# A decoder layer on one core: first expert stage fed in quarters, idle products, kept rows and the first projection blocks rearranged

## The chip, the cores and the metric

The kernel runs on one core of a Trainium2 chip. The metric is the device time of one execution in microseconds (us), as the median over several executions. TensorE is called PE here (its weight loads PEld), VectorE DVE, ScalarE ACT, GpSimd POOL and SyncE SP, as in the profile.

## What is computed

One decoder layer for 256 prompt tokens and 8 sample tokens, 264 together. All data are float32. Cut to what matters here:

```python
h = x + mixer(rmsnorm(x, norm_mix))            # one wide input projection w_in, SSD and short convolution
h = h + cross_attn(rmsnorm(h, norm_xattn), mem)
h = h + moe(rmsnorm(h, norm_moe))              # top 4 of 32 experts
y = rmsnorm(h, norm_final)

def moe(x):                                    # x is normed
    logits = x @ w_router + b_router
    top_v, top_i = top_k(logits, 4)
    gates = softmax(top_v)
    # per expert: gather its tokens, then
    gate, up = split(xb @ w_gate_up[e] + b_gate_up[e])
    y = ((clip(up) + 1) * gate * sigmoid(1.702 * gate)) @ w_down[e] + b_down[e]
    # scatter y * gate weight back to the tokens
```

The last three conv input rows and the sample rows of the projection are outputs too (`new_mconv`, `new_sconv`).

## The kernel before

Activations lie transposed, features on the partitions and the 264 tokens along the free axis: `hT` holds h, `xnT` its normed copy, each as 8 blocks of 128 features. A projection of 128 features is 8 matmuls of 128x264 into one PSUM bank (`project`, L1532); float32 makes two instructions of each. The order of the work on PE, ACT and DVE is written out by hand. `PLAN` (L51 to L93) lists every job of a bank with the engine that empties it; `filled`, `emptied` and `free_bank` turn it into waits.

**Start.** PE runs two idle matmuls of 512 columns (L1507), turns x block by block (a 128-row tile, the 8 sample rows, later the second 128-row tile), turns the parameter rows (`par0`) and spreads the root of the mean squares over the partitions with a product (`rbc`, L1492). DVE makes the sums of squares (L942) and scales the rows by `norm_mix` and the root (L959, `scale_rows`). Then come blocks `xb` 0 to 3, from a weight chunk of 2 MB that is fetched in halves, one from SP's queue (L477) and one from ACT's (L622).

**Router.** PE computes the attention's output projection `xo` in 8 blocks. After block j it adds the router's product of block j-1 (`route`) and turns the raw block back to tokens (`turn_tokens`). The last ones are followed by the sums of squares (`sum_tokens`), from which ACT and DVE make the root (L858, L1325); DVE then makes logits, the top four and a mask (L1329 to L1347). PE counts ranks with triangular products (`rank`, two idle products ahead and three behind, L1946), and in the same bank the total per expert, from which the number of passes follows (`npass`). DVE compares ranks with slot numbers (`select`, L1358): a selection matrix `selT` for 64 slots of each of two experts. `gather` multiplies it with the token rows `xtok` that ACT has scaled, ACT copies the result (`copy_rows`), PE turns it (`turn_rows`) and DVE multiplies by the gains `norm_moe` (`spread`, L1395), which gives `xg`, the stationary side of the expert's matmuls. Meanwhile six sets of four small turns bring out the kept rows (`mrow`, `srow`), which POOL writes to memory.

**Experts.** A pair of experts is 12 stages, one for each chunk of 2 MB: `gate_up(e, part)` four times for each expert, `down(e)` two for each. A stage is 16 matmul instructions of 64x512 columns and ends with an increment of `stage_done`. There are nine slots, so nine chunks (numbers 0 to 8) are fetched ahead. From then on SP fetches chunk after chunk, each when a stage has freed a slot:

```python
for g, done_stages in zip(range(AHEAD, AHEAD + 8), (1, 2, 3, 5, 6, 7, 8, 9)):
    sp.wait_ge(S["stage_done"], done_stages)
    refill(g, g // 12)
```

The slot of chunk 3 is used only once (it is work space later), so stage 4 is not in the list. Inside a pair PE also turns the activations, scatters the previous pair's result, and gathers, turns and biases for the next pair. Of the 16 pairs the first and the last are written out, and the 14 between run in a loop. After the last come a scatter, the final norm and the output.

The names in the rows: `flat` holds x and the parameter rows at the start, `tokT` is `hT` and `xnT`, `wide` is the work space, `ring`, `conv`, `flat`, `tokT` and a part of `wide` are the weight slots. L1492 is the helper for every product, L1503 the one for every turn, L618 and L609 ACT's copies.

## Time and profile before

| what | value |
|---|---|
| runs | 1410.58 us median of 3 (1409.34 to 1411.57) |
| profiled execution | span 1407.9 us; its time outside the span is not given |
| PE | 1376.7 us busy, 98% of the span |
| DVE / ACT / POOL | 441.5 / 217.9 / 27.9 us busy |
| memory read / written | 488.61 MB / 8.24 MB |
| chain that ended last | PE 83%, DMA 14%, DVE 2%, issue 1% |

The span runs from the first to the last instruction of the profiled execution. A busy share is an average over stages with different limits, so it does not name a bound. The chain is followed back from the last instruction, at each step to what released it. PE's records overlap, so the start of the next group is the better end of a group than its own busy time. In a timeline several like instructions in a row stand in one line with their count.

### The profile page before, as it was taken

Reading aid. Unit: us, or ns where it says so; the run is one execution under the profiler, and the core shown is the slowest. Engines: PE = TensorE matmul, PEld = TensorE weight load, DVE = VectorE, ACT = ScalarE, POOL = GpSimd, SP = SyncE. Lnnn points to the kernel's source line nnn. Section 1 sums busy time; section 2 is a strip of 40 time slices with the busy share of each in tenths; the row PEclk is TensorE's granted clock in tenths of the full one; section 3 lists DMA queues with packets and bytes.
Section 4 is the critical chain, followed back from the end, with each engine's and each line's share of the span. In section 5 each row is a group of like instructions: output and inputs, shape, how many; then the busy total and the mean of one; then the engine's idle time right before and its main releaser. Section 6 shows DMA issues by size and latency. Waiting matters only on the chain.

```text
span 1407.9 us, 16140 instructions
## 1 busy us (share of the span) xinstructions
PE 1376.7 (98%) x6438; PEld 673.5 (48%) x6438; DVE 441.5 (31%) x902; ACT 217.9 (15%) x403; POOL 27.9 (2%) x48
## 2 busy tenths in 40 slices
PE   9999999999999999999999999999999999999997
PEld 7788887677757633333333333333333332332322
DVE  5634345871461312221211312212113121121213
ACT  2220022052123411110101111011011010110102
POOL 0000002200000000000000000000000000000000
PEclk9999999999999999999999999999999999999999
DMA  7644446975379799999999999999999999999995
GB/s 256 210 154 154 175 142 200 376 268 190 118 283 398 284 413 428 429 425 430 427 430 427 430 427 429 428 429 429 428 428 429 430 427 430 427 430 426 431 426 228
DMA packets 71575, 497.25 MB, mean 353 GB/s; under 512 B 8752, under 2 KB 10216, under 8 KB 46824
## 3 DMA queue, kind: packets, MB, share of 16 engines
q1 hardware_dynamic: 65180, 477.94, 82.5%
q0 software_dynamic: 4432, 15.53, 3.0%
q10 hardware_dynamic: 1924, 3.23, 0.7%
q8 instruction: 27, 0.44, 0.1%
q14 instruction: 12, 0.10, 0.0%
HBM read 488.61 MB, written 8.24 MB: 353 GB/s over the span
## 4 chain that ended last, share of the span: by engine, by line
PE 83%; DMA 14%; DVE 2%; issue 1%; ACT 0%; SPq 0%; DVEq 0%
PE bank L1492 78%; DMA ring<-in_w_gate_up 8%; DMA flat<-in_w_gate_up 6%; PE bank L1503 4%; DVE wide L1418 1%; DMA flat<-in_x_prompt 0%; DVE wide L1475 0%; ACT wide L618 0%; PE bank L1946 0%; ACT L628 0%; ACT L658 0%; ACT wide L609 0%; SPq L506 0%; DVE wide L1466 0%; DVE wide L1395 0%
## 5 line engine op out<-in xcount | busy, mean ns | idle before, releaser
L1492 PE MATMUL bank<-ring,wide 128*64 128x512 f32 (+2 forms) x1696 | 405.5, 595 | 6.9 <-DMA ring<-in_w_gate_up 6.0
L1492 PE MATMUL bank<-wide 128*64 128x512 f32 (+6 forms) x1024 | 283.3, 574 | 8.7 <-DVE wide L1418 6.3
L1492 PE MATMUL bank<-tokT,ring 128*128 128x264 f32 x1152 | 266.0, 389 | 0.8 <-DVE tokT L959 0.8
L1492 PEld LDWEIGHTS bank<-ring,wide 128*64 128x64 f32 (+2 forms) x1696 | 132.4, 140 | 259.9 <-issue 246.1
L1492 PEld LDWEIGHTS bank<-tokT,ring 128*128 128x128 f32 x1152 | 217.8, 191 | 42.4 <-issue 6.4
L1492 PEld LDWEIGHTS bank<-wide 128*64 128x64 f32 (+4 forms) x1024 | 94.6, 152 | 171.9 <-issue 121.9
L609 ACT ACTIVATE wide<-bank 64x512 f32<-64x512 f32 (+3 forms) x104 | 58.2, 560 | 348.3 <-PE bank L1492 227.0
L1442 DVE TENSOR_SCALAR wide<-bank 128x512 f32<-128x512 f32 x32 | 22.1, 692 | 274.3 <-PE bank L1492 274.3
L1492 PE MATMUL bank<-flat,wide 128*64 128x512 f32 (+2 forms) x408 | 92.3, 589 | 3.7 <-DMA flat<-in_w_gate_up 3.7
L1492 PE MATMUL bank<-conv,wide 128*64 128x512 f32 (+1 forms) x400 | 91.1, 596 | 0.3 <-ACT wide L609 0.3
L890 ACT ACTIVATE wide<-wide 128x512 f32<-128x512 f32 x32 | 20.2, 630 | 428.6 <-DVE wide L1442 428.6
L1492 PE MATMUL bank<-tokT,wide 128*64 128x512 f32 x384 | 86.5, 592 | 0.0
L618 ACT ACTIVATE wide<-bank 128x264 f32<-128x264 f32 (+5 forms) x92 | 42.7, 482 | 210.3 <-PE bank L1492 179.2
L1492 PE MATMUL bank<-wide,ring 128*128 128x264 f32 x256 | 58.4, 386 | 0.5 <-ACT wide L609 0.5
L1492 PEld LDWEIGHTS bank<-flat,wide 128*64 128x64 f32 (+2 forms) x408 | 29.7, 137 | 59.7 <-issue 53.1
L1492 PEld LDWEIGHTS bank<-tokT,wide 128*64 128x64 f32 x384 | 27.6, 137 | 54.8 <-issue 54.8
L1418 DVE TENSOR_TENSOR wide<-bank,wide 8x512 f32<-8x512 f32 x32 | 21.8, 681 | 99.8 <-PE bank L1492 99.6
L1492 PEld LDWEIGHTS bank<-wide,ring 128*128 128x128 f32 x256 | 48.1, 190 | 9.1 <-ACT wide L609 0.7
L1492 PEld LDWEIGHTS bank<-conv,wide 128*64 128x64 f32 (+1 forms) x400 | 26.9, 135 | 53.2 <-issue 52.5
L1503 PEld LDWEIGHTS bank<-ident,wide 128*128 128x128 f32 (+4 forms) x252 | 31.7, 173 | 41.2 <-issue 39.8
L1423 DVE TENSOR_TENSOR wide<-bank,wide 128x512 f32<-128x512 f32 x64 | 44.2, 691 | 17.4 <-PE bank L1492 16.9
L1386 DVE COPY wide<-id 128x128 f32 (+1 forms) x16 | 3.6, 225 | 135.4 <-PE bank L1492 135.4
(257 smaller groups left out, 735.1 us busy)
## 6 DMA issues: line engine op xcount, KB each, us to landing
ring<-in_w_gate_up SPq DMA_DIRECT2D x64, 2048.0 KB, 26.1
ring<-in_w_down SPq DMA_DIRECT2D x32, 2048.0 KB, 28.1
flat<-in_w_gate_up SPq DMA_DIRECT2D x16, 2048.0 KB, 26.9
conv<-in_w_gate_up SPq DMA_DIRECT2D x16, 2048.0 KB, 25.5
wide<-in_w_gate_up SPq DMA_DIRECT2D x16, 2048.0 KB, 25.7
tokT<-in_w_gate_up SPq DMA_DIRECT2D x16, 2048.0 KB, 27.0
ring<-in_w_in SPq DMA_DIRECT2D x15, 2048.0 KB, 12.3
wide<-in_w_down SPq DMA_DIRECT2D x8, 2048.0 KB, 25.2
```

The source lines that it names most:

```text
L609: return s.activation(out, in_, ACT.Copy, scale=scale)
L618: done(s.activation(out, src, func), name, k)
L890: s.activation(sig[:, e, :], gate[:, e, :], ACT.Sigmoid, scale=ALPHA).then_inc(S["sig_ready"], 1)
L1386: v.tensor_copy(onehot[:, buf].rearrange("p (j c) -> p j c", j=2), bc(id4[:, bass.ds(pair * 2, 2)], CAP))\
L1418: ins = v.tensor_tensor(out=acc[0:TS, 2, 512 * h:512 * h + 512] if last else acc[rows, 2, 0:512], in0=bank[5 if last else 6][rows, :], in1 ...
L1423: return v.tensor_tensor(out=dst, in0=bank[j - 1 if last else 6 + j % 2][:, :], in1=dst, op=ALU.add)\
L1442: v.tensor_scalar(gate[:, e, :], bank[2 * e][:, :], LIMIT, None, ALU.min).then_inc(S["g_ready"], 1)
L1492: last[0] = pe.matmul(out, lhsT, rhs, start=start, stop=stop)
L1503: last[0] = pe.transpose(out, in_, ident[0:k, 0:k])
```

## The change

It keeps all results and moves or recasts these pieces:

- Start: a third idle product; the eight rows of `norm_mix` get a transfer, a turn and a copy of their own (`gain`), so that the scaling does not need `par0`; x is turned in blocks with all three tiles, four blocks before the root product and four behind; the second half of the first weight chunk goes through SP's queue; the first four blocks take the first half of the contraction each, then the second half each (`xb_first`).
- Sums: split in two, the part over blocks 0 to 6 before the last routings, the last block's behind; they now write three columns with unit vectors (`units`).
- Chunks 3 and 8 are fetched after `so` 3 and not after `xo` 7 and the sums; for this the squares `sqo` lie elsewhere, for which ACT waits for the v output ahead of its loop, and `gT` and `onehot` have moved.
- The bias products of the first pair, and idle products, fill PE's waits ahead of the ranks; the total has a bank and a place of its own, in the first pair.
- The first gather is a transposed one: `gather_turned` uses blocks of `xtok` as the stationary side and gives `xg` but for the gains, in four quarters of two blocks. One quarter precedes the first stage, three are put between stages 1 to 3. DVE's `spread_quarter` multiplies each by the gains. The other pairs gather as before.
- The kept rows are turned between stages 3 and 6, and the number of passes is loaded into registers behind the first pair.

```diff
-PLAN = [("xT", 8, A_), ("par0", 1, A_), ("rbc", 1, D_), ("xb", 4, A_), ("memT", 2, A_),
+PLAN = [("gain", 1, A_), ("xT", 4, A_), ("rbc", 1, D_), ("xT", 4, A_), ("par0", 1, A_), ("xb", 4, A_), ("memT", 2, A_),
...
-PLAN += [("xo", 5, D_, (0, 1)), ("xtok", 3, A_, (3, 4, 5)), ("xo", 3, D_, (1, 0)), ("mrow", 1, A_, (0,)),
- ("rt", 3, D_, (2, 6, 7)), ("rs", 1, A_, (1,)), ("xtok", 3, A_, (3, 4, 5)), ("mrow", 3, A_, (1, 6, 7)),
- ("srow", 2, A_, (0, 3)), ("rank", 1, D_, (2,))]
+PLAN += [("xo", 5, D_, (0, 1)), ("xtok", 3, A_, (3, 4, 5)), ("xo", 3, D_, (1, 0)),
+ ("rs", 1, A_, (0,)), ("rt", 3, D_, (2, 6, 7)), ("xtok", 3, A_, (3, 4, 5)), ("rank", 1, D_, (6,)),
+ ("total", 1, D_, (4,)), ("mrow", 4, A_, (5, 4)), ("srow", 2, A_, (5, 4))]
...
         if i == 0:
             sp.dma_start(dst[:, 0:4], src[:, 0:4]).then_inc(first_half, 16)
+            sp.dma_start(dst[:, 4:8], src[:, 4:8]).then_inc(slot_full[where], 16)
...
-    for j, name, k in ((2, "so", 1), (4, "so", 1), (5, "so", 3), (0, "so", 3), (1, "xo", 3), (3, "xo", 7)):
+    for j, name, k in ((2, "so", 1), (4, "so", 1), (5, "so", 3), (0, "so", 3), (6, "so", 3), (8, "so", 3), (1, "xo", 3), (3, "xo", 7)):
         filled(sp, name, k)
         first_chunk(FIRST_SLOT.index(j))
-    first_chunk(3)
-    filled(sp, "rs")
-    first_chunk(8)
     filled(sp, "xtok", 5)
     first_chunk(7)
-    sp.wait_ge(S["passes_ready"], 1)
-    n = sp.value_load(npass[0:1, 0:1], min_val=0, max_val=MAXP - 1)
...
     for g, done_stages in zip(range(AHEAD, AHEAD + 8), (1, 2, 3, 5, 6, 7, 8, 9)):
         sp.wait_ge(S["stage_done"], done_stages)
         refill(g, g // 12)
+    sp.wait_ge(S["passes_ready"], 1)
+    n = sp.value_load(npass[0:1, 0:1], min_val=0, max_val=MAXP - 1)
...
+    s.dma_start(stage[0:KB, 2, :], param_rows("norm_mix")).then_inc(gain_in, 16)
     for t, row, name, n in PARAM_ROWS[:6]:
         s.dma_start(stage[row:row + n, t, :], param_rows(name)).then_inc(par0_in, 16)
-    s.dma_start(mslot[0][:, 4:8], WEIGHTS[0][1][:, 4:8]).then_inc(slot_full[0], 16)
...
+    move("gain", 0, small[:, 302:310], KB)
...
-    for t, n in TILES_P:
-        copy(xtok[0:n, t, :], acc[0:n, t, :], rr[0:n, t:t + 1]).then_inc(S["xtok_ready"], 1)
-    for k in range(1, 4):
+    for h in range(2):
+        for t, n in TILES_P:
+            cols = slice(512 * h, 512 * h + 512)
+            copy(xtok[0:n, t, cols], acc[0:n, t, cols], rr[0:n, t:t + 1]).then_inc(S["xtok_ready"], 1)
+    s.wait_ge(S["lg_ready"], 1)
+    s.activation(gts, gts, ACT.Exp).then_inc(S["lg_exp"], 1)
+    for k in range(4):
         move("mrow", k, mrows[k // 2][:, k % 2 * 512:k % 2 * 512 + 512], 512, 11)
     for k in range(2):
         move("srow", k, srows[:, 512 * k:512 * k + 512], 512, 10)
-    s.wait_ge(S["lg_ready"], 1)
-    s.activation(gts, gts, ACT.Exp).then_inc(S["lg_exp"], 1)
...
+            if job == "rbc":
+                emptied(v, "xT", k)
+            ins = v.scalar_tensor_tensor(out=dst[:, k, 0:n], in0=src[:, k, 0:n], scalar=gain(k),
                                          in1=b[:, 0:n], op0=ALU.mult, op1=ALU.mult)
             if k < KB - 1:
                 ins.then_inc(S[out], 1)
...
-    st(ins)
+    done(ins, "rank")
+    emptied(v, "rank")
     v.wait_ge(S["consts_set"], 2)
     select(0)
...
+    def spread_quarter(q, gathered, ready):
+
+        v.wait_ge(S[gathered], q % 2 + 1)
+        v.tensor_tensor(out=xg[:, 2 * q:2 * q + 2, :],
+                        in0=bank[4 + q][:, 0:256].rearrange("p (k n) -> p k n", k=2),
+                        in1=bc(gains[:, 2 * q:2 * q + 2], P), op=ALU.mult).then_inc(S[ready], 1)
+
...
-    for _ in range(2):
+    for _ in range(3):
         pe.matmul(bank[7][:, :], ones[:], ones[:, 0:1].to_broadcast([P, 512]), start=True, stop=True)
...
+    pe.wait_ge(gain_in, 16)
+    b = free_bank(pe, "gain")
+    turn(b[:, 0:KB], stage[0:KB, 2, :])
+    close("gain")
+    for t in (2, 0, 1):
         pe.wait_ge(x_in[t], 16)
...
+    def turn_x(ks):
+
+        for k in ks:
+            b = free_bank(pe, "xT", k)
+            for t, (c, n) in enumerate(TILES):
+                turn(b[:, c:c + n], xtokin[0:n, t, k * P:k * P + P])
+            close("xT", k)
+
+    turn_x(range(4))
     b = free_bank(pe, "rbc")
...
+    turn_x(range(4, KB))
+    pe.wait_ge(par0_in, 16 * 6)
+    b = free_bank(pe, "par0")
+    turn(b[:, 0:P], stage[:, 0, :])
+    close("par0")
...
+    def xb_first():
+
+        for half in range(2):
+            if half:
+                chunk_in(pe, "xb0")
+            else:
+                pe.wait_ge(first_half, 16)
+            for j in range(4):
+                b = bank[BANK[JOB["xb", j]]] if half else free_bank(pe, "xb", j)
+                for k in range(4 * half, 4 * half + 4):
+                    if j == 0:
+                        x_normed(k)
+                    mm(b[:, 0:T], mslot[0][:, k, j * P:j * P + P], xnT[:, k, :], k == 0, k == KB - 1)
+                if half:
+                    close("xb", j)
...
+    def sum_early():
         b = free_bank(pe, "rs")
         pe.wait_ge(S["sq_summed"], 1)
+        for t, (c, n) in enumerate(TILES):
+            mm(b[0:n, 0:3], rinv[:, c:c + n], units[:, 3 * t:3 * t + 3], t == 0, False)
+
...
-        for t, (c, n) in enumerate(TILES):
-            mm(b[0:n, t:t + 1], rinv[:, c:c + n], ones[:, 0:1], True, False)
-            mm(b[0:n, t:t + 1], sqo[:, KB - 1, c:c + n], ones[:, 0:1], False, True)
+        b = bank[BANK[JOB["rs", 0]]]
+        for t in (2, 0, 1):
+            c, n = TILES[t]
+            mm(b[0:n, 0:3], sqo[:, KB - 1, c:c + n], units[:, 3 * t:3 * t + 3], False, t == 1)
         close("rs")
...
+    def stay_warm(b, n):
+
+        pe.matmul(b[:, 0:n], ident[:], bgu[:, 0:n], start=True, stop=True)
...
+        if j == KB - 1:
+            sum_early()
         if j:
             route(j - 1)
-            turn_tokens(j - 1)
-    pe.wait_ge(S["raw_kept"], 1)
-    cache_rows("mrow", 0, kept_x, 11)
+            if j < KB - 1:
+                turn_tokens(j - 1)
+    sum_last()
     route(KB - 1)
-    sum_tokens()
+    stay_warm(bank[1], 512)
+    turn_tokens(KB - 2)
     turn_tokens(KB - 1)
...
+    def gather_turned(h, blocks):
+
+        for i in blocks:
+            out = bank[4 + 2 * h + i // 2][:, i % 2 * P:i % 2 * P + P]
+            for t in (0, 1):
+                rows = xtok[:, t, 512 * h:512 * h + 512].rearrange("p (s d m) -> p s m d", d=P, m=2)
+                mm(out, rows[:, i // 2, i % 2, :], selT[:, t, :], t == 0, False)
+            rows = slice(32 * h, 32 * h + TS)
+            ends = xtok[rows, 2, 0:512].rearrange("p (s d m) -> p s m d", d=P, m=2)
+            mm(out, ends[:, i // 2, i % 2, :], selT[rows, 2, :], False, True)
...
     pe.wait_ge(S["crossed_in"], 96)
-    hidden_bias(first_pair, 0)
...
+    hidden_bias(first_pair, 0, (0,))
+    emptied(pe, "rt", 2)
+    stay_warm(bank[7], 512)
+    emptied(pe, "xtok", 3)
+    hidden_bias(first_pair, 0, (1,))
+    pe.wait_ge(S["mask_ready"], 1)
+    b = free_bank(pe, "rank")
...
+    close("rank")
+    stay_warm(bank[7], 512)
+    stay_warm(bank[7], 128)
+    emptied(pe, "xtok", 4)
+    pe.wait_ge(S["sel_ready"], 1)
+    pe.wait_ge(S["xtok_ready"], 3)
+    gather_turned(0, (0, 1))
+    last[0].then_inc(S["xg_gathered"], 1)
+    stay_warm(bank[7], 256)
...
+        if first:
+            pe.wait_ge(S["xg_quarter"], 1)
+            gate_up(0, 0)
+            emptied(pe, "xtok", 5)
+            gather_turned(0, (2, 3))
+            last[0].then_inc(S["xg_gathered"], 1)
+            emptied(pe, "rank")
+            pe.wait_ge(S["xtok_ready"], 5)
+            gather_turned(1, (0, 1))
+            last[0].then_inc(S["xgt_turned"], 1)
+            pe.wait_ge(S["xg_quarter"], 2)
+            gate_up(0, 1)
+            gather_turned(1, (2, 3))
+            last[0].then_inc(S["xgt_turned"], 1)
+            pe.wait_ge(S["xg_ready"], 1)
+            gate_up(0, 2)
+            b = free_bank(pe, "total")
+            for t, (_, r) in enumerate(TILES):
+                mm(b[:, 0:E], ones[0:r, :], msk[0:r, t], t == 0, t == 2)
+            close("total")
+            pe.wait_ge(S["raw_kept"], 1)
+            cache_rows("mrow", 0, kept_x, 11)
+            cache_rows("mrow", 1, kept_x, 11)
+            pe.wait_ge(S["xg_ready"], 2)
+            gate_up(0, 3)
+            cache_rows("mrow", 2, kept_x, 11)
+            cache_rows("mrow", 3, kept_x, 11)
+            gate_up(1, 0)
+            pe.wait_ge(S["cv_kept"], 1)
+            cache_rows("srow", 0, kept_cv, 10)
+            cache_rows("srow", 1, kept_cv, 10)
+            gate_up(1, 1)
...
     experts(first_pair, 0, 0, first=True)
+    pe.wait_ge(S["passes_ready"], 1)
+    n = pe.value_load(npass[0:1, 0:1], min_val=0, max_val=MAXP - 1)
```

PE at the start, before: the idle products, the turns and the root product, up to the first blocks.

```order
L1507 MATMUL bank<-ones 128x512 x2
L1503 MATMUL bank<-ident,flat 128x8
L1503 MATMUL bank<-ident,flat 128x128
...
L1503 MATMUL bank<-ident,flat 128x128 x10
L1492 MATMUL bank<-ident,rtok 128x128 x2
L1492 MATMUL bank<-ident,rtok 128x8
L1492 MATMUL bank<-tokT,ring 128x264 x32
```

The turns end with the parameter rows, and the root product follows them all.

PE at the start, in the changed kernel. The 8-row `stage` turn and the turns of `flat` by threes:

```order
L1527 MATMUL bank<-ones 128x512 x3
L1523 MATMUL bank<-ident,flat 128x8
L1523 MATMUL bank<-ident,flat 128x128 x2
L1523 MATMUL bank<-ident,flat 128x8
...
L1512 MATMUL bank<-ident,rtok 128x128 x2
L1512 MATMUL bank<-ident,rtok 128x8
L1523 MATMUL bank<-ident,flat 128x128 x2
...
L1523 MATMUL bank<-ident,flat 128x8
L1523 MATMUL bank<-ident,flat 128x128
L1512 MATMUL bank<-tokT,ring 128x264 x32
```

The root product stands between two groups of turns, and the parameter turn is last.

PE from the ranks to the first stages, before (`ustr` and `ones` products are the ranks and the total, `xgt` turns are `turn_rows`, `ring,wide` 64x512 are stages):

```order
L1946 MATMUL bank<-bgu,ident 128x256 x2
L1492 MATMUL bank<-wide,ustr 128x32
L1492 MATMUL bank<-wide,ones 128x32
L1492 MATMUL bank<-wide,ustr 128x32
L1492 MATMUL bank<-wide,ones 8x32 x2
L1492 MATMUL bank<-wide,ustr 8x32
L1492 MATMUL bank<-wide,ones 128x32 x3
...
L1492 MATMUL bank<-wide 128x512 x6
...
L1503 MATMUL bank<-ident,xgt 128x128 x8
...
L1492 MATMUL bank<-ring,wide 64x512 x24
L1492 MATMUL bank<-wide 64x512 x8
L1492 MATMUL bank<-ring,wide 64x512 x8
```

Six stages follow each other without other work.

PE at the same place in the changed kernel:

```order
L1986 MATMUL bank<-bgu,ident 128x512
L1986 MATMUL bank<-bgu,ident 128x128
L1512 MATMUL bank<-wide 128x128 x6
L1986 MATMUL bank<-bgu,ident 128x256
L1512 MATMUL bank<-ring,wide 64x512 x8
L1512 MATMUL bank<-wide 128x128 x12
L1512 MATMUL bank<-ring,wide 64x512 x8
L1512 MATMUL bank<-wide 128x128 x6
L1512 MATMUL bank<-ring,wide 64x512 x8
L1512 MATMUL bank<-wide,ones 128x32 x3
L1523 MATMUL bank<-ident,kept 11x128 x8
L1512 MATMUL bank<-wide 64x512 x8
```

The six 512-column products and eight turns are gone; 24 products of 128x128 stand for them, six of them ahead of the first stage and 18 between stages, where the total and the kept rows follow.

SP's queue from the first expert chunk to the first refill, before:

```order
L484 DMA ring<-in_w_gate_up 128x4096
L484 DMA flat<-in_w_gate_up 128x4096
L484 DMA conv<-in_w_gate_up 128x4096
L484 DMA ring<-in_w_gate_up 128x4096 x3
L484 DMA wide<-in_w_gate_up 128x4096
L484 DMA wide<-in_w_down 128x4096
L484 DMA tokT<-in_w_gate_up 128x4096
L501 TENSOR_LOAD npass
...
L506 DMA ring<-in_w_down 128x4096 x3
```

The two `wide` chunks (3 and 8) come behind all `ring` chunks but the refills.

SP's queue at the same place in the changed kernel:

```order
L486 DMA ring<-in_w_gate_up 128x4096
L486 DMA flat<-in_w_gate_up 128x4096
L486 DMA conv<-in_w_gate_up 128x4096
L486 DMA ring<-in_w_gate_up 128x4096
L486 DMA wide<-in_w_gate_up 128x4096
L486 DMA wide<-in_w_down 128x4096
L486 DMA ring<-in_w_gate_up 128x4096 x2
L486 DMA tokT<-in_w_gate_up 128x4096
L503 DMA ring<-in_w_down 128x4096 x3
```

The two `wide` chunks (3 and 8) stand ahead of the last two `ring` chunks, and the load of `npass` has left this place.

## Rows read from the trace of the kernel before

**Rows 1.** The page: transfer rate in 40 slices of the span.

```profile
GB/s 256 210 154 154 175 142 200 376 268 190 118 283 398 284 413 428 429 425 430 427 430 427 430 427 429 428 429 429 428 428 429 430 427 430 427 430 426 431 426 228
```

**Rows 2.** The chain of waits: start us, us, what.

```profile
558.43 0.99 PE bank L1492 x4
...
615.10 0.99 PE bank L1492 x4
...
1071.84 0.99 PE bank L1492 x4
...
1130.57 0.99 PE bank L1492 x4
...
1361.19 3.65 PE bank L1492 x16
```

**Rows 3.** Timeline of SP's queue: start us, us, then the instruction.

```profile
489.43 7.20 SPq L506 DMA_DIRECT2D ring<-in_w_down  x3
...
525.02 0.33 SPq L506 DMA_DIRECT2D wide<-in_w_gate_up  x1
```

**Rows 4.** Windows: PE, PEld, DVE, ACT, POOL busy; clock; DMA share; GB/s.

```profile
524.00:526.00 2.00, 2.00 (x12) 0.67 (x10) 0.00 (x0) 0.00 (x0) 0.00 (x0) 1.00 0.78 320
526.00:528.00 2.00, 2.00 (x12) 0.57 (x8) 0.00 (x0) 0.00 (x0) 0.00 (x0) 1.00 0.94 254
```

**Rows 5.** Timeline of the start, all engines.

```profile
1.08 3.78 PE L1507 MATMUL bank<-ones 128*128 128x512 f32 x4 [1.08 <-POOL ones L535]
...
5.71 0.38 PEld L1503 LDWEIGHTS bank<-ident,flat 8*128 8x128 f32 x2 [0.22 <-issue]
...
6.40 1.23 DVE L942 CUSTOM_DVE_ANT_0 conv<-flat 128x1024 f32<-128x1024 f32 x1
...
8.27 0.13 DVE L952 RECIPROCAL rtok<-rtok 8x1 f32<-8x1 f32 x1
...
13.45 3.29 DVE L959 SCALAR_TENSOR_TENSOR tokT<-tokT,par,bank 128x264 f32<-128x264 f32 x8 [5.05 <-PE bank L1492]
...
14.08 16.13 PE L1492 MATMUL bank<-tokT,ring 128*128 128x264 f32 x64 [0.76 <-DVE tokT L959]
```

**Rows 6.** Groups by form, PE, 14.1-17.6 us, then 18-30 us: busy us.

```profile
L1492 PE MATMUL bank<-tokT,ring 128*128 128x264 f32 x9 | 3.9, 610 | 0.8 <-DVE tokT L959 0.8
...
L1492 PE MATMUL bank<-tokT,ring 128*128 128x264 f32 x55 | 12.4, 386 | 0.0
```

**Rows 7.** Timeline of PE, routing to stage 6, and ACT's root.

```profile
467.33 0.68 PE L1492 MATMUL bank<-wrt,tokT 128*128 128x32 f32 x6
...
470.65 0.26 ACT L858 ACTIVATE wide<-bank,eps 128x2 f32<-128x2 f32 x1 [1.10 <-PE bank L1492]
...
471.10 2.64 PE L1503 MATMUL bank<-ident,kept 128*11 128x128 f32 x20
473.57 1.03 PE L1946 MATMUL bank<-bgu,ident 128*128 128x256 f32 x4
474.87 0.41 PE L1492 MATMUL bank<-wide,ustr 128*128 128x32 f32 x2 [0.27 <-DVE wide L1347]
...
476.02 0.96 PE L1492 MATMUL bank<-wide,ones 128*128 128x32 f32 x6
...
478.41 4.76 PE L1492 MATMUL bank<-wide 8*128 8x512 f32 x12
...
485.73 10.52 PE L1492 MATMUL bank<-ring,wide 128*64 128x512 f32 x48 [0.37 <-DVE wide L1395]
...
506.49 0.75 PE L1503 MATMUL bank<-ident,wide 128*128 128x128 f32 x4
```

**Rows 8.** One line, L477: issue ns, first and last start us.

```profile
L477 SPq DMA_DIRECT2D ring<-in_w_in x1: 429/429/429, 2.2 to 2.2; - x1
...
DMA to landing us min/median/max: 10.9/10.9/10.9
```

**Rows 9.** Timeline of PE, dense matmuls of 128x128.

```profile
212.36 3.84 PE L1492 MATMUL bank<-wide,flat 128*128 128x128 f32 x32
```

164 lines of the change are left out of this document (65 added, 99 removed).

## Prediction

> **What bounds the kernel now.** I read the page first: TensorE (PE) is busy nearly all the time and the transfer rate sits at 425 to 431 GB/s from about the middle of the program on [rows 1]. Two full resources at once say nothing about which one ends the program, so the chain of waits comes next. In the expert loop four marker rows of the chain give the length of one pair of experts: 615.10 - 558.43 = 56.67 us early and 1130.57 - 1071.84 = 58.73 us late [rows 2]. The early value is the PE's own length. The late one is the weights': a pair is 12 chunks of 2 MB, 25.17 MB, and 25.17 MB in 58.73 us is 428.5 GB/s, the plateau of rows 1; one chunk takes 4.894 us. So the transfers lose 2.06 us per pair against the PE, the nine chunks loaded ahead are used up after some eight pairs, and from then on a shift of the stream of transfers is a shift of the end. The last long stretch of PE work starts at 1361.19 on a chunk that had just landed [rows 2], with six chunks still to come: 1361.2 + 6 x 4.9 = 1390.6.
>
> What sets the stream's place? A chunk may be fetched when a stage (one chunk's worth of matmuls) frees its slot. Stage 1 frees the first at 489.43, stage 9 frees the eighth at 525.02 [rows 3]. Stage 1 would allow the eighth chunk to start at 489.43 + 7 x 4.894 = 523.69; it is allowed only at 525.02, 1.33 us later. The finely cut windows show that hole: 320 and then 254 GB/s from 524 to 528 where 429 is normal, (109 + 175) x 2 / 429 = 1.3 us lost [rows 4]. Check: 525.02 + 2.0 until data flows + 176 x 4.894 = 1388.4, and the last chunk was issued early enough that only the queue holds it. **So the end follows stage 9 of the first pair**, by up to 1.33 us it could follow stage 1 instead, and every later pair has 2.06 us more slack.
>
> **The change part by part.** The sum is made against the profiled execution, whose span is 1407.9 us; the median of the three runs is 2.7 us above that span, and I carry that difference unchanged. About 0.2% (2.8 us) is what a measurement of this kernel can tell from no change.
>
> *Start.* Between 14.08 and 30.21 the PE does 64 matmul instructions for the first four blocks [rows 5]. The first of them run at 3.9 / 9 = 0.43 us each, the rest at 12.4 / 55 = 0.225 us [rows 6]: 264 columns in the one and the other are TensorE's levels of 1.2 and 2.4 GHz. The column of the granted clock reads 1.00 for the whole stretch, so I go by the durations. Before the rise at about 17.8 the PE had run four warming instructions (1.08 to 4.9) and then transposes with gaps: 0.38 us of weight loads and 0.22 us idle for each pair of a 128-row and an 8-row turn [rows 5]. After 3.7 us of dense matmuls the rate doubled. The change puts a third warming matmul in (six instructions at 0.853 us, until 1.08 + 5.1 = 6.2) and ends it just where the second prompt tile is used (6.40 on VectorE, DVE). If the clock rises within this stretch and stays, the turns go at the 2.47 / 20 = 0.12 us that twenty turns take later, 471.10 to 473.57 [rows 7], about 0.48 us for a block's three; four blocks end at 6.5 + 1.9 = 8.4, just as the root is ready (8.27 + 0.13) [rows 5]; the root's product takes 0.7 (half of the 1.4 or so that it takes before DVE starts at 13.45); the other four blocks and the parameters end at 11.2. The scaling on DVE needs only the eight columns of the new small parameter transfer and starts about 9.3 instead of 13.45, so it is ahead. 64 instructions at 0.2225 us are 14.24: end at 25.5, 4.7 us earlier than 30.21. The bound on the other side is the weights: the first half chunk landed at 2.2 + 10.9 = 13.1 [rows 8]. If it does so again, the gain is 30.21 - 13.1 - 14.24 = 2.9. The other half no longer competes from ScalarE's (ACT's) queue but follows it on SP's, so I expect it near 11.5 and take **-4.2**, ends -2.9 and -4.7. The new split order (half the contraction for four blocks, then the other half) has 7.1 us of work before it needs the second half. SP issues one transfer more here, 0.43 us [rows 8], under transfers that are needed much later. From here to the router the chain is PE nearly without gaps, so I let the shift arrive whole.
>
> The Trainium skill (page "TensorE: Matmul & The Clock Gate", Part 1) says that half rate is the default state, that sustained activity lifts it, and that the same kernel reaches full rate after differing numbers of matmuls from run to run. The trace agrees with the first two parts (0.43, then 0.225 us). By the last part the median would lie between this case and the next, as no one profile decides.
>
> *Router to first stage.* I count from the routing matmuls at 467.33. ACT reads the row sums at 470.65, 3.3 us in [rows 7]; the change puts them ahead of the last routing block, one set of turns and one set of kept rows, so they are read about 2.0 in. From there to the first rank matmul lie 474.87 - 470.65 = 4.2 us, less one 0.18 us subtraction taken off DVE's chain: 6.1 in, about when the PE has done its bias products (moved here, about 1 us) and two warming matmuls. The ranks take 1.15 (474.87 to 476.02) and no longer share their bank with the total, 0.96 us [rows 7]; DVE needs 1.3 for ranks and selection (as before, 478.41 less the 477.1 at which it began): selection at 8.7. ACT's scaled rows are ready about 0.3 earlier, so they do not hold it. The gather changes form: six 512-column matmuls, copies on ACT, eight turns and two scalings, 478.41 to 485.73 or 7.3 us, become for the first weights a quarter of a transposed gather. 128x128 matmuls take 3.84 / 32 = 0.12 us an instruction [rows 9]; a quarter is 12, so 1.4 to 1.5, and its scaling 0.5 with its waits. The first expert matmul then stands 10.7 in, against 485.73 - 467.33 = 18.4: **stage 1 comes 7.7 us earlier**.
>
> Stage 9 still has all of that work before it. Before, stage 6 ends at 506.49 - 467.33 = 39.2. Now: 10.7, the six stages' 20.8 (485.73 to 506.49), three quarters of the gather (4.3), the total (0.8), 24 turns of kept rows (2.8), and five interruptions of the stream at about 0.2 (chosen; a switch between forms shows a tenth or two at each side): 40.4, or 1.2 late. From stage 6 to 9 nothing changes. If the interruptions are free and a quarter takes 1.2, it is 0.5 early; at 0.4 each it is 2 late. I take **+1.0**, ends -0.5 and +2.0.
>
> *Other pieces.* Two chunks (3 and 8) are asked for two projections earlier; by the argument above chunks before the eighth refill do not set the end: 0. If that cover is gone, the stage that waits for chunk 3 pays its landing, not seen before. The pass count is loaded to a register behind the first pair instead of ahead of it, on PE, ACT, DVE and SP. On PE it now lies between two pairs, under 2.06 us of slack; before, it fitted with the last turns and the scaling into the time to 485.73, so it is far below that: 0. ACT now waits for the v output before its first square; it is asked for before the sample's values are weighed, well ahead of the output projection, so I count 0; if it were late, everything behind would wait.
>
> **Sum:** -4.2 + 1.0 = -3.2: span 1404.7, runs **1407.4**.
>
> **The rivals.** *The clock does not rise at the start.* Four warming instructions did not lift it before; six may not. Then the turns keep 0.78 us a block, the products 1.4, and the PE reaches the weights at about 14.3; with 16.13 as before it ends 0.2 us later. With the router's +1.0 this is +1.2: 1411.8. For it: after the four instructions the turns ran at half rate all the same [rows 5]. Against: the stretch is half as long again, 5.1 us, and the rise at 17.8 came after no more dense work than that.
>
> *Stage 1 sets the stream.* If the interruptions cost nothing and the first pair closes up, stage 9 moves by its end of -0.5 or better by 1.5, and with the whole 4.7 in front the sum is -6.7: 1403.9. More than that only if the eighth refill did not need stage 9; the 1.3 us hole speaks against.
>
> *The pieces cost more than the gather they replace (slower).* Eight of the transposed gather's 24 matmuls, 16 instructions, use 8 rows. At the start an 8-row weight load is followed by 0.22 us of idle time [rows 5]. If each of the 16 pays this, 16 x 0.22 = 3.5 us come on top in the first pair, stage 9 is 4.5 us late and, with no clock gain (+0.2), the sum is +4.7: 1415.3. It decides, past 0.2%, as soon as the pieces cost 1.6 us more than I count and the start gains nothing. Against it: the 0.22 is a low-clock value, and half of it at full clock leaves 1413.5.
>
> **How the numbers follow.** Forecast 0.54 (own range 1405.0 to 1409.2, of it 0.37 beyond 0.2%, as its span crosses 1407.8); clock stays low 0.25 (0.24 within); stage 1 0.08 (faster); pieces 0.13 (0.12 slower). That gives faster 0.45, same 0.42, slower 0.13. The range 1404.0 to 1412.3 takes in the forecast and the low clock with 0.5 us of noise, and leaves out most of the last two, 0.18.
>
> **What would show it.** Start: the first 264-column matmul near 11.5 and all at 0.22 us; the fourth block done near 26 (at 30.4 the clock rival is right). Router: stage 1's refill 7 to 8 us nearer to the last routing block. Decisive: the refill by stage 9 at 525.0 - 4.2 + 1.0 = 521.8, the hole in front of it larger than 1.3 us, and the end moved by the same amount. If the end moves by another amount than this refill, the argument on the stream is wrong; if stage 9 is earlier than the start alone explains, the cost of the pieces is.

## The result, and the profile after

The changed kernel takes 1416.71 us (median of 5, 1415.01 to 1417.95) against 1410.58 of the kernel before (median of 5): ratio 1.0037, 95% interval 1.0026 to 1.0048. It is **slower by 6.1 us of medians** (5.2 by the ratio), where 3.2 faster was forecast and 1412.3 was the range's upper end. The profiled span is 1414.1 against 1407.9. From here on the run times of profiled executions are known too: they lie 1.9 to 2.1 us above their spans.

The page of the kernel after shows the plateau of [rows 1] again, 426 to 430 GB/s from the 17th slice to the last but one. The chain of waits of the kernel after (start us, us, what) answers to [rows 2]:

```profile
564.03 0.98 PE bank L1512 x4
...
620.70 0.98 PE bank L1512 x4
...
1078.01 0.99 PE bank L1512 x4
...
1136.77 0.98 PE bank L1512 x4
...
1367.38 3.65 PE bank L1512 x16
```

A pair is again 56.67 us early and 58.76 late; only the whole is shifted, the last stretch by 1367.38 - 1361.19 = 6.2 us. So the time is lost before the expert loop. The timeline of SP's queue after (start us, us, instruction), for [rows 3]:

```profile
483.90 14.06 SPq L503 DMA_DIRECT2D ring<-in_w_down  x3
...
530.62 0.33 SPq L503 DMA_DIRECT2D wide<-in_w_gate_up  x1
```

Stage 1 frees its slot 5.5 us earlier than before (489.43), stage 9 frees its own 5.6 us **later** (525.02), and the end went with stage 9. The windows around that refill (PE, PEld, DVE, ACT, POOL busy; clock; DMA share; GB/s), for [rows 4]:

```profile
528.00:530.00 2.00, 2.00 (x13) 0.59 (x10) 0.00 (x0) 0.00 (x0) 0.00 (x0) 1.00 0.69 295
530.00:532.00 2.00, 2.00 (x12) 0.70 (x10) 0.00 (x0) 0.00 (x0) 0.00 (x0) 1.00 0.59 115
532.00:534.00 2.00, 2.00 (x11) 0.49 (x7) 0.00 (x0) 0.00 (x0) 0.00 (x0) 1.00 0.70 238
534.00:536.00 2.00, 2.00 (x13) 0.91 (x13) 0.59 (x2) 1.19 (x2) 0.00 (x0) 1.00 1.01 434
```

Against 429 the hole is (134 + 314 + 191) x 2 / 429 = 3.0 us, where it was 1.3. What stage 1 allowed early is lost at once: all chunks ahead were in by then and the transfers stood nearly still from 480 to 484 (37 GB/s on average), had little to do again from 490 to 492 (123 GB/s), before stage 2 was done, and waited again here.

The start of the kernel after, timeline of all engines, for [rows 5]:

```profile
1.07 4.82 PE L1527 MATMUL bank<-ones 128*128 128x512 f32 x6 [1.07 <-POOL ones L534]
...
4.10 12.24 SPq L439 DMA_DIRECT2D wide<-in_mem_prompt  x2
...
6.54 2.13 PE L1523 MATMUL bank<-ident,flat 128*128 128x128 f32 x12 [0.50 <-DMA flat<-in_x_prompt]
...
11.98 14.51 PE L1512 MATMUL bank<-tokT,ring 128*128 128x264 f32 x64
...
28.52 1.58 PE L1523 MATMUL bank<-ident,wide 128*128 128x128 f32 x8 [2.03 <-DMA wide<-in_mem_prompt]
```

The start went as forecast in this profile: twelve turns in 2.13 us and 64 products in 14.51 (0.227 each), done at 26.5 instead of 30.2. (Whether the third warming matmul did it is another question, see "The start in the other profiles".) Then PE stands 2.03 us for the memory tokens, which SP's queue takes 12.24 us to issue, and the router's first row begins at 467.55, no earlier than the 467.33 of before.

The router and the first stages, timeline of PE after, for [rows 7]:

```profile
467.55 0.63 PE L1512 MATMUL bank<-wide,rinv 128*128 128x3 f32 x6
...
470.02 1.13 PE L1986 MATMUL bank<-bgu,ident 128*128 128x512 f32 x2
470.98 0.82 PE L1523 MATMUL bank<-ident,tokT 128*128 128x128 f32 x6
471.73 1.09 PE L1512 MATMUL bank<-bgu,wide 32*64 32x512 f32 x8
472.75 1.13 PE L1986 MATMUL bank<-bgu,ident 128*128 128x512 f32 x2
473.80 1.09 PE L1512 MATMUL bank<-states,wide 32*64 32x512 f32 x8
474.82 0.41 PE L1512 MATMUL bank<-wide,ustr 128*128 128x32 f32 x2
...
477.41 2.23 PE L1512 MATMUL bank<-wide 128*128 128x128 f32 x12
479.57 0.70 PE L1986 MATMUL bank<-bgu,ident 128*128 128x256 f32 x2
480.20 3.65 PE L1512 MATMUL bank<-ring,wide 128*64 128x512 f32 x16
483.79 4.45 PE L1512 MATMUL bank<-wide 128*128 128x128 f32 x24
488.17 3.65 PE L1512 MATMUL bank<-ring,wide 128*64 128x512 f32 x16
491.75 2.26 PE L1512 MATMUL bank<-wide 128*128 128x128 f32 x12
493.94 3.65 PE L1512 MATMUL bank<-ring,wide 128*64 128x512 f32 x16
497.52 0.96 PE L1512 MATMUL bank<-wide,ones 128*128 128x32 f32 x6
498.42 1.04 PE L1523 MATMUL bank<-ident,kept 128*11 128x128 f32 x8
```

The two halves of the bias products take 1.02 us each (471.73 to 472.75, 473.80 to 474.82); both together took 1.05 before (483.09 to 484.14). A quarter of the gather takes 2.16 (477.41 to 479.57), the other three 4.38 and 2.19. Stage 6 ends at 512.1, 44.5 us behind the first row, where it was 39.2.

### The profile page after: what moved, and what is told of

It is laid out like the page before. It is cut to its first block, busy times and chain, and to the rows that moved or that the text cites. A ratio compares the mean times of both kernels' runs of the same rounds, so it can differ in the third digit from the quotient of the medians.

```text
span 1414.1 us, 16187 instructions
## 1 busy us (share of the span) xinstructions
PE 1381.7 (98%) x6469; PEld 675.5 (48%) x6469; DVE 442.3 (31%) x906; ACT 217.8 (15%) x404; POOL 27.9 (2%) x48
## 4 chain that ended last, share of the span: by engine, by line
PE 82%; DMA 15%; DVE 1%; issue 1%; SPq 1%; ACT 0%; DVEq 0%
PE bank L1512 77%; DMA ring<-in_w_gate_up 8%; DMA flat<-in_w_gate_up 6%; PE bank L1523 4%; DMA wide<-in_mem_prompt 1%; DVE wide L1435 1%; SPq L439 1%; PE bank L1986 0%; DVE wide L1495 0%; ACT wide L617 0%; ACT L627 0%; ACT L658 0%; ACT wide L608 0%; SPq L429 0%; SPq L503 0%
## 5 line engine op out<-in xcount | busy, mean ns | idle before, releaser
L1512 PE MATMUL bank<-wide 128*64 128x512 f32 (+7 forms) x1066 | 288.3, 560 | 9.0 <-DVE wide L1435 6.3
L1512 PEld LDWEIGHTS bank<-wide 128*64 128x64 f32 (+4 forms) x1066 | 100.2, 153 | 173.1 <-issue 121.2
L1435 DVE TENSOR_TENSOR wide<-bank,wide 8x512 f32<-8x512 f32 x32 | 21.8, 681 | 100.4 <-PE bank L1512 100.2
L1474 DVE COPY wide<-bank 128x264 f32<-128x264 f32 x16 | 6.9, 433 | 122.6 <-PE bank L1523 122.6
## 6 DMA issues: line engine op xcount, KB each, us to landing
flat<-in_w_gate_up SPq DMA_DIRECT2D x16, 2048.0 KB, 27.2
ring<-in_w_in SPq DMA_DIRECT2D x15, 2048.0 KB, 12.2
```

The costliest lines, as they stand in the source:

```text
L1435: ins = v.tensor_tensor(out=acc[0:TS, 2, 512 * h:512 * h + 512] if last else acc[rows, 2, 0:512], in0=bank[5 if last else 6][rows, :], in1 ...
L1474: v.tensor_copy(gT, bank[4][:, 0:T]).then_inc(S["gT_ready"], 1)
L1512: last[0] = pe.matmul(out, lhsT, rhs, start=start, stop=stop)
```

## The experiments

Each was timed 5 to 12 times beside the kernel before, whose median was 1411.79 beside the first four, 1410.51 beside the next four (rows_side to kept_in_waits), 1410.89 beside three_costs and 1410.48 beside the other three; the ratios are taken against those runs, and a median in the table is not to be subtracted from 1410.58. Time and granted clock vary together: the twelve runs of start_only go from 1408.50 us at a mean granted clock of 0.999 to 1414.25 at 0.992. The marks below come from one profile each. Eight kernels (after, kept_quarter, rows_side, bias_whole, no_idle, kept_in_waits, ends_together, three_costs) do the same up to the root, and it stands at 467.76 to 470.63; so a mark by itself is uncertain by up to 3 us, and the distances between marks of one profile are what the readings rest on. "Root" is ACT's read of the row sums, "ranks" PE's first rank product, "S1" and "S9" the refills by stages 1 and 9, all in us of the profile.

| kernel | median | ratio to before, 95% | root | ranks | S1 | S9 | span | span - S9 |
|---|---|---|---|---|---|---|---|---|
| before | 1410.58 | | 470.65 | 474.87 | 489.43 | 525.02 | 1407.9 | 882.9 |
| after | 1416.71 | 1.0037 (1.0026, 1.0048) | 469.50 | 474.82 | 483.90 | 530.62 | 1414.1 | 883.5 |
| start_only | 1411.04 | 0.9994 (0.9983, 1.0005) | 469.42 | 473.64 | 488.20 | 523.78 | 1407.1 | 883.3 |
| router_only | 1416.08 | 1.0033 (1.0022, 1.0044) | 469.95 | 475.27 | 484.35 | 531.08 | 1414.1 | 883.0 |
| start_mem_act | 1411.49 | 0.9996 (0.9983, 1.0009) | 468.35 | 473.81 | 488.27 | 523.85 | 1407.1 | 883.3 |
| kept_quarter | 1415.39 | 1.0023 (1.0012, 1.0033) | 469.85 | 475.17 | 484.25 | 529.51 | 1412.7 | 883.2 |
| rows_side | 1415.01 | 1.0028 (1.0016, 1.0040) | 469.04 | 474.36 | 483.35 | 529.75 | 1412.8 | 883.1 |
| bias_whole | 1415.61 | 1.0037 (1.0024, 1.0050) | 470.63 | 474.76 | 483.84 | 530.56 | 1413.6 | 883.0 |
| no_idle | 1419.29 | 1.0065 (1.0053, 1.0078) | 470.38 | 474.44 | 487.32 | 534.04 | 1417.2 | 883.2 |
| kept_in_waits | 1415.44 | 1.0038 (1.0025, 1.0051) | 468.17 | 472.97 | 483.69 | 529.43 | 1412.4 | 883.0 |
| ends_together | 1414.04 | 1.0026 (1.0015, 1.0037) | 467.76 | 473.08 | 481.76 | 527.33 | 1411.2 | 883.9 |
| three_costs | 1411.44 | 0.9994 (0.9983, 1.0005) | 468.12 | 473.93 | 482.62 | 526.72 | 1409.9 | 883.2 |
| sums_first | 1409.92 | 0.9998 (0.9988, 1.0007) | 468.21 | 472.44 | 489.23 | 524.81 | 1407.9 | 883.1 |
| sums_first_mem | 1407.65 | 0.9984 (0.9972, 0.9996) | 466.71 | 471.79 | 486.25 | 521.83 | 1405.2 | 883.4 |

**What sets the end.** Read the last column first: over 14 kernels S9 ranges over 12.2 us and the span stays 882.9 to 883.9 behind it. S1 does not do that: in start_only and three_costs S1 is 5.6 us apart in one direction and the spans 2.8 in the other. These runs separate stage 9 from stage 1 but not from its neighbours, since S9 follows the end of stage 6 by 18.4 to 18.5 us in all of them; that it is stage 9 rests on the hole just before its refill. That it is the stream of transfers and not PE alone rests on the late pairs, 58.76 us against PE's own 56.67.

### The two halves of the change

start_only is the kernel before with the change's start, router_only the changed kernel without it. Of the pieces exchanged, as start_only has them:

```diff
-            for _ in range(2):
+            for _ in range(3):
...
+            pe.wait_ge(gain_in, 16)
...
+            turn_x(range(4))
...
-            xb(0, 1, 2, 3)
+            xb_first()
...
-            s.dma_start(mslot[0][:, 4:8], WEIGHTS[0][1][:, 4:8]).then_inc(slot_full[0], 16)
```

> The start of the change alone, on the router and the first pair of before. Theory A (the four blocks end 3.7 us earlier, but the memory tokens land at 28.5 and the turns that follow wait for them, and the block behind them runs at the lower clock again): every marker from 60 us on stands 0.2 us later than before, time within 1 us of before (1410 to 1412). Rival (the start does give 3 to 4 us and the router takes 9 to 10): 1406.5 to 1407.5.

> All of the change but its start. Theory A: the refill by stage 9 comes 5.4 us later than before and so does the end, 1415.5 to 1417. Rival (a large part of the 6.1 us is the start's): below 1413.5.

router_only carries the loss: 4.3 us by its median against the runs beside it (1416.08 and 1411.79), a ratio of 1.0033 where the whole change has 1.0037, and 6.2 us of span. Its S9 is 6.1 us later in time and, as expected, 5.4 counted from the router's first row (468.00). start_only is 0.75 us faster by its median, and its interval takes in no change; its profile has S9 1.2 us earlier. Timeline of PE in start_only:

```profile
12.19 14.41 PE L1496 MATMUL bank<-tokT,ring 128*128 128x264 f32 x64
28.78 1.09 PE L1507 MATMUL bank<-ident,wide 128*128 128x128 f32 x8 [2.19 <-DMA wide<-in_mem_prompt]
```

The same stop as in the changed kernel. Before, PE came to these turns at 30.05, when the memory tokens had landed; now it is there at 26.6 and they are not.

### The start in the other profiles

The new start stands in 12 of the 14 kernels. Timeline of PE at the start, before, then router_only (which has the old start and its two warming matmuls), then bias_whole (new start, three):

```profile
5.14 6.81 PE L1503 MATMUL bank<-ident,flat 8*128 8x8 f32 x25 [0.28 <-DMA flat<-in_x_prompt]
...
4.98 4.76 PE L1519 MATMUL bank<-ident,flat 8*128 8x8 f32 x24
...
15.60 15.97 PE L1512 MATMUL bank<-tokT,ring 128*128 128x264 f32 x64
```

In router_only two warming matmuls were followed by turns at full rate (24 in 4.76 us, where 25 took 6.81; a weight load of 0.14 us from 5.56 on, where before shows 0.18), and the clock was back at 0.50 from 9 us to 19. In bias_whole, no_idle and rows_side three warming matmuls did not hold it: PE waited 1.6, 1.6 and 0.7 us for the prompt (but 0.96 in kept_quarter, where the clock stayed at 1.00), the clock fell to 0.50 at 8 to 10 us, and the fourth block ended at 31.4, 31.2 and 29.8. In the other nine it ended at 26.3 to 27.2. So the full rate came in nine profiles of twelve and half rate, as the clock rival has it, in three, and no run takes the third warming matmul alone: that it lifts the clock is not shown. The landing of the memory tokens is why it hardly matters: rows_side ended its four blocks 3.3 us behind the changed kernel and has its root 0.5 us ahead of it (469.04 against 469.50).

### The memory tokens on another queue

```diff
-                        sp.dma_start(memv[t], a["mem_prompt"][0, t * P:(t + 1) * P, :].rearrange("p (a n) -> p a n", a=4))\
-                            .then_inc(mem_in, 16)
...
+                s.dma_start(memv[t], a["mem_prompt"][0, t * P:(t + 1) * P, :].rearrange("p (a n) -> p a n", a=4))\
+                    .then_inc(mem_in, 16)
```

> start_only with the two transfers of the memory tokens moved from SP's queue, behind two weight chunks, to ACT's. Theory A (what takes the start's gain is the landing of the memory tokens): they land well before 26.5, the four blocks end near 26.5, PE goes on at the full clock and the end is 3.5 to 4 us earlier than before, 1406.6 to 1407.1. Rival (the memory system gives no more bytes by then, whatever the queue: the next chunk is late instead): gain under 1.5 us, with PE waiting for the second chunk.

Here `sp` is SP's queue, where they stood behind the first weights, and `s` ACT's, where they stand behind the parameter rows. Missed in the median, met by the lowest of 12 runs alone (1406.71); by its median the rival is nearer, with the wait for `wdt` in place of the one for a chunk. The stop at 26 us is gone, a smaller one takes its place, 1.42 us for `wdt` at 36.7. The root stands 2.30 us earlier than before against 1.23 in start_only, so the memory tokens were worth 1.07 there. Behind it the ranks came 5.46 us after the root instead of 4.22, with the granted clock at 0.50 from 470 to 472, so 1.2 us went again. Why the clock fell is not shown: PE was busy 1.88 of the 2 us before.

### What stage 9 has ahead of it

kept_quarter leaves out three quarters of the kept rows:

```diff
-                for i in range(4):
+                for i in range(1):
                     turn(b[0:n, i * P:i * P + P], src[:, 4 * k + i, :])
```

> The changed kernel with one turn of four in each of the six sets of kept rows (the other three quarters of those output rows are left out): 18 turns fewer between stages 3 and 6 of the first pair, 18 x 0.12 = 2.2 us. Stage 1 keeps its place. Theory A (the eighth refill, by stage 9, sets the end): refill and end both 2.2 us earlier than in the changed kernel, 1414.5. Rival (stage 1 or an earlier refill sets the end): the end does not move, 1416.7.

From the ranks to S9 it is 54.34 against 55.80: 1.46 us less, of 2.2 expected. The turns take 1.19 us instead of 2.90 (two sets of one turn still cost 0.32, the first two 0.55), and 0.26 comes back as a wait for DVE at the end of stage 6. S1 kept its place (1.46 of S9 - S1 as well) and the span went with S9. By the runs alone this would not be shown: the intervals of the ratios (1.0012 to 1.0033, and 1.0026 to 1.0048 for the changed kernel) overlap, and so do those of rows_side, bias_whole, kept_in_waits and ends_together; there too the marks carry the reading. Those of no_idle and three_costs lie clear.

rows_side asks whether the strided weight load makes the gather's products slow:

```diff
-                    copy(xtok[0:n, t, cols], acc[0:n, t, cols], rr[0:n, t:t + 1]).then_inc(S["xtok_ready"], 1)
+                    copy(side(xtok[0:n, t, cols]), apart(acc[0:n, t, cols]), rr[0:n, t:t + 1]).then_inc(S["xtok_ready"], 1)
...
-                        rows = xtok[:, t, 512 * h:512 * h + 512].rearrange("p (s d m) -> p s m d", d=P, m=2)
+                        rows = xtok[:, t, 512 * h:512 * h + 512].rearrange("p (s m d) -> p s m d", d=P, m=2)
```

> The changed kernel with ACT writing the scaled token rows in the order in which the transposed gather reads them, so that each 128x128 weight block is contiguous instead of every second element; same result. A quarter of the gather is 12 instructions and took 2.16 us (0.18 each) where 128x128 products in the input stage take 0.12. Theory A (the strided weight load is what makes it 0.18): a quarter takes 1.5 us, the first stage comes 0.7 us earlier, stage 9's refill 2.6 us earlier counted from the last routing block, and the end moves by the same: 1416.7 - 2.6 = 1414.1. Theory B (0.18 is the price of a 128-column weight load with only 128 columns streamed behind it and of the switches of output, whatever the stride): the quarter stays 2.16 and the time 1416.7. Ends: if ACT's permuted reads are slower than its plain ones, the first stage is late by up to 0.5 us.

Theory B, nearly: a quarter takes 2.08 instead of 2.16, the whole gather 8.41 instead of 8.73. The stride is worth 0.3 us, not 2.6. (Ranks to S9 is 55.39, 0.4 less; the last 0.1 lies behind stage 6.)

ends_together changes the order, and with it the flags that open and close the sum in a bank:

```diff
-                for i in blocks:
-                    out = bank[4 + 2 * h + i // 2][:, i % 2 * P:i % 2 * P + P]
+                outs = [bank[4 + 2 * h + i // 2][:, i % 2 * P:i % 2 * P + P] for i in blocks]
+                for i, out in zip(blocks, outs):
...
-                        mm(out, rows[:, i // 2, i % 2, :], selT[:, t, :], t == 0, False)
+                        mm(out, rows[:, i // 2, i % 2, :], selT[:, t, :], i == blocks[0] and t == 0, False)
+                for i, out in zip(blocks, outs):
...
-                    mm(out, ends[:, i // 2, i % 2, :], selT[rows, 2, :], False, True)
+                    mm(out, ends[:, i // 2, i % 2, :], selT[rows, 2, :], False, i == blocks[-1])
```

> The changed kernel with the products of the transposed gather in another order: in each call the 128-row products of all its blocks first and then the 8-row products of all its blocks, so that the row count changes twice a call and not twice a block; same result. In the changed kernel six instructions of a block take 1.09 us, with 0.11 between like ones and 0.2 at each change of the row count. Theory A (the change of row count is what costs): a block is 0.2 us cheaper, a quarter 1.76 instead of 2.16, the first stage 0.2 to 0.4 and stage 9's refill 1.6 us earlier counted from the last routing block: 1415.1. Theory B (the eight-row instructions cost 0.3 us each wherever they stand): a quarter stays at 2.16, 1416.7.

Timeline of PE in ends_together:

```profile
475.67 1.84 PE L1512 MATMUL bank<-wide 128*128 128x128 f32 x12
477.44 0.70 PE L1986 MATMUL bank<-bgu,ident 128*128 128x256 f32 x2
...
481.65 3.67 PE L1512 MATMUL bank<-wide 128*128 128x128 f32 x24
485.26 3.65 PE L1512 MATMUL bank<-ring,wide 128*64 128x512 f32 x16
```

**Theory A, in the marks.** A quarter takes 1.77, two take 3.61 instead of 4.38, ranks to S9 54.25, 1.55 less than 55.80 for eight changes between 128 and 8 rows less: 0.19 us each. (The median is 1414.04, of 1415.1 expected.) In the changed kernel the eight blocks change 16 times: 48 instructions at 0.115 are 5.5 us, 16 changes 3.1, together 8.6 of the 8.7 measured. The Trainium skill (page "TensorEngine Tiling (Array Packing)", Key Properties) says that changing the tiling mode, not just the tile, drains TensorE. It gives no price, and that an 8-row weight block is such another mode is a reading that no run here shows; the 0.19 us does not speak against it.

### What stands ahead of the ranks

```diff
-            hidden_bias(first_pair, 0, (0,))
             emptied(pe, "rt", 2)
             stay_warm(bank[7], 512)
             emptied(pe, "xtok", 3)
-            hidden_bias(first_pair, 0, (1,))
+            hidden_bias(first_pair, 0)
```

> The changed kernel with the bias products of both experts in one call again, at the later of the two places. Theory A: the two halves take 1.02 us each, as much as both together before, and the second stands in front of the ranks, so the ranks, the first stage and stage 9's refill all come 1.0 us earlier: 1415.7. Theory B: the ranks wait for the mask that DVE makes, not for PE; then they move by less, 0.3 us or nothing: 1416.5.

Root to ranks is 4.13 against 5.32: 1.19 us less, and all of it arrives at S9, counted from the root. Timeline of PE in bias_whole:

```profile
473.72 0.66 PE L1512 MATMUL bank<-bgu,wide 32*64 32x512 f32 x4
473.74 0.66 PE L1512 MATMUL bank<-states,wide 32*64 32x512 f32 x4
...
474.76 0.41 PE L1512 MATMUL bank<-wide,ustr 128*128 128x32 f32 x2
```

The products of the two experts start 0.02 us apart, and 16 instructions take 1.04 us (473.72 to 474.76) where 8 alone take 1.02: they run side by side. By the kernel each of the eight products has its own 32 of the rows and 64 of the output columns. Split into two calls, with an idle product between, they did not overlap. (The median is 1.1 lower as well, but the ratio is the same 1.0037: in this profile the start ran at half rate and the root stands 1.1 us later.)

no_idle removes all five `stay_warm` calls of the changed kernel. kept_in_waits keeps the first and puts kept rows in the place of three, with banks 7 and 5 for them:

```diff
-            stay_warm(bank[7], 512)
+            pe.wait_ge(S["raw_kept"], 1)
+            cache_rows("mrow", 0, kept_x, 11)
             emptied(pe, "xtok", 3)
...
-            stay_warm(bank[7], 512)
-            stay_warm(bank[7], 128)
+            emptied(pe, "xtok", 5)
+            cache_rows("mrow", 1, kept_x, 11)
...
-            stay_warm(bank[7], 256)
```

> The changed kernel without its five idle products between the routing and the first stage. Theory A (the idle products are in PE's way: the two 512-column ones take 1.13 and 1.05 us where PE would otherwise wait for less): ranks, first stage and stage 9's refill come 1.3 us earlier, 1415.4. Theory B (they keep the clock up): without them the granted clock falls in the waits and the first stage runs at half rate, 3 us and more later: 1419 or above, visible as 0.43 us and more an instruction of 64x512 at twice that.

> The changed kernel with two of the six sets of kept-row turns put back into PE's waits, one in place of the second idle product, one in place of the third pair, and the 256-column idle product behind the first quarter dropped. Theory A (stage 9's refill sets the end, and useful work outside the waits is what the change added to it): two sets less between the stages are 1.0 us, a set is 0.5 us shorter than the idle product that it replaces ahead of the ranks, so the first stage comes 0.5 and stage 9's refill 1.5 us earlier: 1415.2. Theory B (the first stage sets the stream): only 0.5: 1416.2.

no_idle met its theory B. The ranks come 1.26 us sooner behind the root (4.06), and then (windows of no_idle, the clock is the last column but two):

```profile
474.00:476.00 2.00, 1.22 (x12) 0.99 (x12) 0.58 (x5) 2.00 (x4) 0.00 (x0) 0.93 0.99 422
476.00:478.00 2.00, 0.97 (x4) 0.93 (x4) 1.05 (x5) 1.98 (x3) 0.00 (x0) 0.50 1.00 426
...
484.00:486.00 2.00, 2.00 (x8) 0.67 (x6) 0.00 (x0) 0.00 (x0) 0.00 (x0) 0.51 0.00 0
486.00:488.00 2.00, 2.00 (x11) 0.82 (x8) 0.00 (x0) 0.00 (x0) 0.00 (x0) 1.00 0.00 0
```

PE waited 1.07 us before the ranks and 1.37 behind them, and with that second wait the clock goes to 0.50, the level of 1.2 GHz, for about ten microseconds; the first stage takes 5.86 us instead of 3.59. The idle products of the change are not waste: without them the median is 1419.29 and the ratio 1.0065. But they do not always hold the clock, as three_costs shows below. kept_in_waits showed the same in a smaller dose and no theory of mine had it: ranks 0.5 us sooner as expected, then waits of 0.84 and 0.52 us around the first quarter, and the first stage at the lower clock:

```profile
475.56 2.23 PE L1513 MATMUL bank<-wide 128*128 128x128 f32 x12 [0.84 <-DVE wide L1367]
478.31 5.34 PE L1513 MATMUL bank<-ring,wide 128*64 128x512 f32 x16 [0.52 <-DVE wide L1397]
```

That took 1.7 us, more than the 1.0 the two sets give back: ranks to S9 56.46, and the ratio stayed at 1.0038.

### Three costs at once

three_costs has the edits of bias_whole, ends_together and kept_quarter together.

> The changed kernel with three costs taken out at once: the bias products in one call, the gather's 8-row products together at the end of each call, and one kept-row turn of four in each set (this leaves out three quarters of the kept rows). Counted from ACT's root of the router to stage 9's refill, the three alone gave 1.2, 1.55 and 1.45 us off 61.1. Theory A (they stand one behind the other on PE, which sets stage 9, and stage 9 sets the end): together 4.2 off, 56.9, and with a span 883.3 above the refill's time the median comes to 1416.7 - 4.2 = 1412.5. Theory B (a wait on DVE, ACT or the clock comes in their place when all are gone, or the first stage begins to set the stream): 2 to 3 off, 1414.

From the ranks to S9 it is 52.79: 3.01 less than 55.80, exactly the 1.55 of ends_together and the 1.46 of kept_quarter. Root to ranks was 5.81, not 4.13, because the granted clock was 0.50 from 470 to 472 in the profiled execution (two idle products of 512 columns took 1.73 us where they take 1.13), although the idle products were there and PE's records show no gap from 466 on (up to 468.6 they are products of 264, 3 and 32 columns, as in the other kernels). The median is 1411.44, 1.1 better than expected, at the time of the kernel before; S9 in the profile is 3.9 us earlier than in the changed kernel, of 4.2 expected. (This kernel, too, leaves out three quarters of the kept rows, so it is no replacement.)

### A kernel made of the parts that pay

sums_first is start_only with one part of the router: the row sums in two parts, ahead of the last routing block; all kept rows behind them, in the wait for the mask; one set in the wait behind the ranks; no split of the bias, old gather.

```diff
+                if j == KB - 1:
+                    sum_early()
...
+            sum_last()
+            route(KB - 1)
+            turn_tokens(KB - 2)
+            turn_tokens(KB - 1)
             pe.wait_ge(S["raw_kept"], 1)
             cache_rows("mrow", 0, kept_x, 11)
-            route(KB - 1)
-            sum_tokens()
-            turn_tokens(KB - 1)
...
-            cache_rows("srow", 1, kept_cv, 10)
-            emptied(pe, "xtok", 5)
-            stay_warm(2)
             pe.wait_ge(S["mask_ready"], 1)
...
-            stay_warm(3)
+            cache_rows("srow", 1, kept_cv, 10)
+            emptied(pe, "xtok", 5)
+            stay_warm(2)
```

> The kernel before with the change's start and, of the router, only the sums of squares: taken in two parts as in the change and ahead of the last routing block, with the kept-row turns behind them in the wait for the mask (the idle products there are gone, the last set of turns stands in the wait behind the ranks). Old gather, bias products in one call, all six sets of turns ahead of the first stage. Theory A (stage 9's refill sets the end; what stands in a wait of PE is free, what stands outside costs its length): against the kernel with the new start alone, the ranks, the first stage and stage 9's refill all come 1.2 us earlier, refill at 522.6 and 1.2 + 0.7 = 1.9 us off the kernel before: 1408.6. Theory B (the chain over ACT and DVE needs the time anyway, or the clock falls in the wait without idle products): ranks not earlier, 1409.8 or later.

> The kernel of sums_first with the memory tokens on ACT's queue, so that PE does not wait for them at 26 us. That brought the root of the router 1.1 us further forward (468.35 against 469.42), and its profile lost this again behind the routing. Theory A: with PE dense there it arrives: stage 9's refill near 521.5 and 1407.5. Theory B: the clock falls again behind the routing and the time is that of sums_first, 1408.6 or above.

sums_first: ranks 1.2 us earlier as expected (472.44 against 473.64), but the turns behind the ranks waited 0.63 us for ACT to empty their bank and the clock fell to 0.50 from 476 to 478 (0.81 and 0.84 in the 2 us before and after): S9 came at 524.81, the median at 1409.92. That is theory B's second half. sums_first_mem had PE denser at this place in its profile (ranks at 471.79, gather at 475.22, clock 1.00 from 474 to 478), S9 at 521.83 and 1407.65: **0.9984 of the kernel before (0.9972 to 0.9996)**, by medians 2.8 us less than the kernel before beside it and 9.1 less than the changed one. The interval leaves out no change, but the gain is below the 0.2% that the prediction set as what can be told, and against sums_first (0.9988 to 1.0007) the intervals overlap. Of the 3.0 us that S9 gains over sums_first, 1.5 are there at the root; the rest is where the clock happened to fall, in this profile between root and ranks (0.50 from 468 to 470, 5.08 us instead of 4.23) and not behind the ranks.

## Why the prediction was wrong

- **What sets the stream: right.** "So the end follows stage 9 of the first pair" held in all 14 profiles, and an earlier stage 1 gave nothing. This was the decisive reading, and the wrong forecast came from its two inputs.
- **"I let the shift arrive whole": wrong, 4.4 us.** The start's own part came near: the fourth block ended at 26.5, against 25.5 worked out and 26.0 as taken (first half chunk in at 11.95, 11.5 expected). But I checked cover only for the weights. A gain of 3.7 us at a PE that is never waiting means that every transfer behind it must be 3.7 us early too; the memory tokens landed at 28.5, `wdt` was the next. Alone the start gave 1.2 in its profile and 0.75 in the medians. In the changed kernel's own profile even that is gone: the wait for the memory tokens was followed by a granted clock of 0.50 from 30 to 32 us, and the block there took 4.97 us where start_only's took 3.73. In start_only the same wait (2.19 us) was followed by a clock of 1.00, so the clock's part is not bound to the wait. The 4.4 is that one profile's: over the eight kernels with the same code the root stands at 469.2 on average, and in router_only, with the old start, at 469.95, so the start was worth about 0.8 us there too, not 4.2.
- **The clock at the start: half luck.** The sum took the rise of the clock for sure and gave its absence 0.25. It came in nine profiles of twelve, and came once with the old start, so "Four warming instructions did not lift it before" was the reading of one profile.
- **"a quarter is 12, so 1.4 to 1.5": the term that was mis-sized.** I priced a quarter at 1.4 to 1.5 by a row with 128-row products alone [rows 9] and put the 8-row ones into a rival with chance 0.13. Measured: 2.16, and 6.57 for three quarters instead of 4.3. That rival's number, 16 x 0.22 = 3.5, was close to the 16 x 0.19 = 3.1 of the runs, in part by luck: it counted 16 instructions where the runs show a price for each of 16 changes, and whether the idle time at the start is the same cost is not shown. "half of it at full clock" was too low. The sum should have carried it. That rival read 1415.3, 1.4 below what came; its gather was right, but its start gained nothing because of the clock, while the real one had the clock and lost the gain at the memory tokens.
- **"about when the PE has done its bias products (moved here, about 1 us)": wrong, 1.2 us.** I kept the price of the whole while the diff split it. The ranks came 7.3 us in, not 6.1, and the first stage 12.65, not 10.7: 1.2 from this and 0.7 from the first quarter. (The selection "at 8.7" adds up to 8.55 from its own terms; the 0.15 more changes nothing here.)
- **The interruptions of the stream: right.** 21.5 us for six stages and five interruptions against 21.8; total 0.90 and kept rows 2.91 as counted. Together 12.65 + 6.57 + 21.51 + 0.90 + 2.91 = 44.5, against 40.4 predicted: 4.1 off, and the two points above make 4.2 of it.
- **Other pieces at 0:** nothing speaks against it, but no run takes them alone.

The sum: +6.2 of span instead of -3.2 is 9.4 us; 4.4 are the start, 4.4 the router (+5.4 at the mark of S9 counted from the first routing mark, instead of +1.0; 0.2 of this is the step from the 1.2 worked out to the +1.0 taken), and 0.6 is the span's distance from S9. That last part stays open, and is within the 1.0 by which this distance varies over the profiles; a longer standstill of the transfers before the refill may need longer to fill again, but ends_together with the shorter gather has the largest distance of all.

## What to carry to other kernels

Find the one slot release that places the stream of transfers, and price a rearrangement by what stands **ahead of that release**; a first stage that starts 5.5 us sooner is worth nothing if its work is moved in front of the ninth. A gain at an engine that never waits is limited by the next transfer it will meet, so list the landings behind the gain before letting it arrive whole. Price an instruction with its neighbours: products that run side by side lose that when they are split, and products with different row counts cost a change each, so sort them by row count. And do not read the state of the clock from one profile: the same start ran at full rate in nine profiles and at half rate in three.

## What the runs showed of the hardware

- A change between 128-row and 8-row weight blocks cost 0.19 us at full clock (ends_together, eight changes fewer: 1.55 us); contiguous instead of strided weights gave 0.3 us over 48 instructions (rows_side).
- Bias products of two experts started 0.02 us apart; 16 instructions took 1.04 us together (bias_whole) and 8 took 1.02 alone (after).
- The granted clock is not a matter of PE's waits alone. It fell to 0.50 for ten microseconds after waits of 1.07 and 1.37 us in no_idle, but also in three_costs and sums_first_mem where PE's records show no gap in the 2 us before it fell (0.50 from 470 to 472 and from 468 to 470; they were products of 264, 3 and 32 columns, and turns), and it stayed at 1.00 after a wait of 2.19 us in start_only.
- At the start the turns ran at full rate behind two warming matmuls in router_only and at half rate behind two in the kernel before; with three the 64 products took 14.4 to 14.5 us in nine profiles and 15.7 to 16.0 in three.
- SP was held 12.24 us by the issue of two transfers of 512 KB behind 4 MB of weights (10.96 in the kernel before, behind 3 MB). On ACT's queue their issue took 1.92 us and they came in time, and small transfers on SP's were held instead (start_mem_act: `norm_mem` 8.65 us for one issue, `wdt` 6.42, `dtb` 7.52).
